# Values of A at the reached half of the far pages' keys only, and those pages' keys read in an order with that half first

## The reference

```
DIL_CFG = ((128, 1), (512, 4), (2048, 16))          # (window, dilation)
for win, dil in DIL_CFG:
    steps = jnp.arange(win // dil + 1) * dil
    kidx = q_idx[:, None] - steps[None, :]          # the keys of this config
    s = einsum(q, k_all[:, kidx]) + bias; s = where(kidx >= 0, s, -inf)
    outs.append(softmax(s) @ v_all[:, kidx])        # then mixed by the denominators
```

## Time and profile before

| | |
|---|---|
| runs | 1401.77, 1408.39, 1410.2 us; median 1408.39 |
| profiled execution | span 1405.5 us, first to last instruction |
| TensorE busy | 1297.9 us, 92% |
| VectorE, ScalarE busy | 550.0 and 257.8 us |
| moved by DMA | 363.80 MB, mean 259 GB/s |

### The profile page before, as it was taken

The page is one execution under the profiler, slowest core; times in us unless marked ns, Lnnn a source line. Parts: engine busy times, 40 slices in busy tenths (PEclk is TensorE's granted clock), DMA queues, the critical chain, the costliest instruction groups (busy, mean ns, idle before and its releaser), DMA issues.

```text
span 1405.5 us, 23104 instructions
## 1 busy us (share of the span) xinstructions
PE 1297.9 (92%) x8038; PEld 816.1 (58%) x8038; DVE 550.0 (39%) x1416; ACT 257.8 (18%) x647; POOL 60.0 (4%) x265
## 2 busy tenths in 40 slices
PE   5989898988899999999999999997879999999998
PEld 2544356645566666666666544665446667767775
DVE  1103787886554101011122088788746511100113
ACT  0111123322213110000004112433211310000001
POOL 1000000000001000000001000000000100000000
PEclk9989999999899999999999999999989999999999
DMA  9988989999843768877863686999993456776663
GB/s 348 239 270 268 284 272 378 322 296 349 283 150 112 274 241 287 316 276 254 333 230 130 202 298 210 332 377 334 348 356 130 142 205 217 242 258 234 210 209 135
DMA packets 189566, 363.80 MB, mean 259 GB/s; under 512 B 22912, under 2 KB 140360, under 8 KB 187786
## 3 DMA queue, kind: packets, MB, share of 16 engines
q1 hardware_dynamic: 155040, 345.62, 71.4%
q10 hardware_dynamic: 34410, 16.70, 4.9%
HBM read 354.17 MB, written 58.40 MB: 294 GB/s over the span
## 4 chain that ended last, share of the span: by engine, by line
PE 67%; DVE 8%; SPq 8%; DMA 7%; DVEq 4%; issue 3%; ACT 2%; ACTq 0%
PE psf L1055 21%; PE psf L1489 19%; SPq L519 7%; DMA ring<-in_tiles 5%; PE psf L1355 4%; PE psf L1401 3%; DVEq L1675 3%; PE psf L1472 3%; DVE m L1672 3%; PE psf L1072 3%; PE psf L1362 2%; PE psf L1102 1%; PE psf L1290 1%; DMA big<-in_pool_cv 1%; PE psf L1134 1%
## 5 line engine op out<-in xcount | busy, mean ns | idle before, releaser
L1055 PE MATMUL psf<-hT,ring 128*128 128x320 f32 x1184 | 329.3, 437 | 2.9 <-DMA ring<-in_tiles 2.7
L1055 PEld LDWEIGHTS psf<-hT,ring 128*128 128x128 f32 x1184 | 224.0, 191 | 111.9 <-issue 15.1
L1489 PE MATMUL psf<-big,ring 128*128 128x320 f32 x1024 | 278.8, 433 | 2.6 <-DVE big L1908 2.1
L1489 PEld LDWEIGHTS psf<-big,ring 128*128 128x128 f32 x1024 | 193.5, 190 | 88.8 <-issue 4.6
L1908 DVE TENSOR_TENSOR big<-sq 128x320 f32<-128x320 f32 x64 | 31.5, 492 | 248.5 <-ACT sq L1024 248.3
L1587 DVE TENSOR_SCALAR rstd<-psf,adaT 128x256 f32<-128x256 f32 x32 | 15.4, 482 | 248.5 <-PE psf L1489 233.3
L1247 PE MATMUL psf<-big,qs 128*32 128x512 f32 x512 | 73.7, 664 | 10.8 <-DVE sel L1877 7.1
L1362 PE MATMUL psf<-hT,ring 128*128 128x320 f32 x224 | 70.3, 459 | 12.2 <-DVE nmxi L1792 12.2
L1672 DVE MAX8 m<-workbuf 64x8 f32<-64x1032 f32 x64 | 78.5, 1227 | 3.5
L1674 DVE MATCH_REPLACE8 workbuf<-m,workbuf 64x1032 f32<-64x1032 f32 x64 | 77.4, 1209 | 0.0
L1355 PE MATMUL psf<-oT,ring 128*128 128x320 f32 x256 | 71.6, 435 | 2.5 <-DMA ring<-in_tiles 1.1
(11 more groups left out here) (192 smaller groups left out, 1255.6 us busy)
## 6 DMA issues: line engine op xcount, KB each, us to landing
ring<-in_tiles SPq DMA_DIRECT2D x272, 512.0 KB, 4.7
big<-in_cache_a SPq DMA_DIRECT2D x64, 768.0 KB, 7.4
out_cache_a<-in_cache_a SPq DMA_DIRECT2D x64, 768.0 KB, 5.8
big<-in_pool_bk SPq DMA_DIRECT2D x128, 192.0 KB, 4.9
big<-in_pool_bv SPq DMA_DIRECT2D x128, 192.0 KB, 6.5
big<-in_pool_cv SPq DMA_DIRECT2D x192, 64.0 KB, 5.9
big<-in_pool_ck SPq DMA_DIRECT2D x128, 64.0 KB, 4.6
big<-in_pool_ck ACTq DMA_DIRECT2D x128, 64.0 KB, 5.3
```

The lines of the kernel that those rows point to most:

```text
L1055: ins = pe.matmul(ps[:, 0:T], ring[:, s, k, :], rhs[:, k, :], start=k == 0, stop=k == KD - 1)
L1489: ins = pe.matmul(bank[6 + m % 2][:, 0:T], ring[:, s, k, :], uT[:, KD * q + k, :], start=q + k == 0, stop=q == 3 and k == KD - 1)
```

## The change

Two things are changed for units of A, in both layers.

First, the values of pages 0 to 3 are loaded in another row order: of each 128 keys first those with a number modulo 16 of 0, then 1, and so on (`reached_first`). For A only the first 64 of these are loaded, on partitions 0 to 63, so this transfer has half the bytes. For C, whose group needs all keys, all 128 rows are loaded in the new order.

Second, everything that meets these values has to be in that order. The logits of pages 0 to 3 are computed with the keys read in it: the moving operand of four matmuls takes a step of 16 elements, in place of adjacent ones. The bias of A, with its mask, is rearranged once, in layer 0, by five copies on VectorE. The outputs of pages 0 to 3 are matmuls over 64 rows for the three groups of A and over 128 for C.

```diff
--- before.py
+++ after.py
@@ -190,6 +190,16 @@
 
     qt, g = n % 2, (6, 0, 1, 2, 7, 3, 4, 5)[n // 2]
     return qt, g, (P if qt == 0 else TP), (2 if g < 6 else 4)
+
+
+
+
+FAR_PAGES = 4
+
+
+def reached_first(ap):
+
+    return ap.rearrange("(a q) w -> q a w", q=16)
 
 
 def repeat(ap, n):
@@ -513,11 +523,11 @@
                                                                  skip_runtime_bounds_check_because=why)
                 return at
 
-            def load_pages(l, at, pool, w0, dst, signal, which=range(NPG)):
+            def load_pages(l, at, pool, w0, dst, signal, which=range(NPG), turned=0):
 
                 for j in which:
-                    sp.dma_start(dst[:, j, :], pool[ds(at[j] + l * N_PHYS, 1), :, w0:w0 + dst.shape[2]]
-                                 .rearrange("o p w -> (o p) w")).then_inc(signal, 16)
+                    src = pool[ds(at[j] + l * N_PHYS, 1), :, w0:w0 + dst.shape[2]].rearrange("o p w -> (o p) w")
+                    sp.dma_start(dst[:, j, :], reached_first(src) if j < turned else src).then_inc(signal, 16)
 
             def load_ik(l, b):
                 load_pages(l, pages(b, CHECKED if l else None), a["pool_ik"], 0, ik[b], ld_ik[b])
@@ -526,16 +536,18 @@
 
                 for e in fours:
                     n, at = A_W // 2, (K_AT, V_AT_)[half]
-                    sp.dma_start(kv[:, u.s, at + n * e:at + n * e + n],
-                                 a["cache_a"][l * NB + u.b, :, half * A_W + n * e:half * A_W + n * e + n]
-                                 ).then_inc((ld_k, ld_v)[half][u.s], 16)
+                    src = a["cache_a"][l * NB + u.b, :, half * A_W + n * e:half * A_W + n * e + n]
+                    dst = kv[:, u.s, at + n * e:at + n * e + n]
+                    if half == 1 and e == 0:
+                        src, dst = reached_first(src)[0:8], dst[0:64]
+                    sp.dma_start(dst, src).then_inc((ld_k, ld_v)[half][u.s], 16)
 
             def load_b(l, u, at, half):
                 load_pages(l, at, a["pool_bv" if half else "pool_bk"], 0, (k_in, v_in)[half][u.s], (ld_k, ld_v)[half][u.s])
 
             def load_c(l, u, at, half, which=range(NPG)):
                 load_pages(l, at, a["pool_cv" if half else "pool_ck"], P * u.second, (ck_in, cv_in)[half][u.s],
-                           (ld_ck, ld_cv)[half][u.s], which)
+                           (ld_ck, ld_cv)[half][u.s], which, FAR_PAGES if half and not u.second else 0)
 
             row = REP * NDIST
 
@@ -1241,6 +1253,8 @@
                             if q < 2:
                                 rhs = (k_in[u.s][:, 4 * q:4 * q + 4, P * c:P * c + P] if c < 3
                                        else ck_in[u.s][:, 4 * q:4 * q + 4, :])
+                                if q == 0 and not u.second:
+                                    rhs = rhs.rearrange("p j (a q) -> p j q a", q=16)
                             else:
                                 rhs = zT[:, u.k + c if c < 3 else u.kc, t0:t0 + NT]
                             masked = u.second and c < 3
@@ -1282,8 +1296,9 @@
                     for j in range(NPG + 1):
                         for c in range(4):
                             if j < NPG:
-                                lhs = PT[:, j, G * c:G * c + G]
-                                rhs = v_in[u.s][:, j, P * c:P * c + P] if c < 3 else cv_in[u.s][:, j, :]
+                                rows = slice(0, 64 if j < FAR_PAGES and c < 3 and not u.second else P)
+                                lhs = PT[rows, j, G * c:G * c + G]
+                                rhs = v_in[u.s][rows, j, P * c:P * c + P] if c < 3 else cv_in[u.s][:, j, :]
                             else:
                                 v0 = u.v + P * c if c < 3 else u.vc
                                 lhs, rhs = PT[0:TS, j, G * c:G * c + G], vs[0:TS, v0:v0 + P]
@@ -1748,6 +1763,14 @@
                         if l == 0:
 
                             dve.wait_ge(ld_dist, N_DIST)
+                            far = slice(0, P * FAR_PAGES)
+                            dve.tensor_copy(S[:, 0, far], sbias[0][:, far])
+                            dve.drain()
+                            for j in range(FAR_PAGES):
+                                page = slice(P * j, P * j + P)
+                                dve.tensor_copy(sbias[0][:, page].rearrange("p (q a) -> p a q", q=16),
+                                                S[:, 0, page].rearrange("p (a q) -> p a q", q=16))
+                            dve.drain()
                         read_logits(UNIT[0])
                     while taken < (made - START[l] - PAIRS) * 2:
                         take8()
```

## The result

| | before | after |
|---|---|---|
| median of the runs timed together | 1407.22 us | 1437.48 us |
| lowest to highest | 1401.77 to 1410.2 | 1433.32 to 1439.48 |
| ratio, with 95% interval | | 1.0228 [1.0199, 1.0257] |
| span of the profiled execution | 1405.5 us | 1431.5 us |

The account below looks back on a forecast made before the run. TensorE, with almost no slack in A units, was taken as the bound, not the loads. Row changes after slack +12.3, bias +0.4 and clock -2.9 us sum to +9.8 on 1408.4, so 1418 us; range 1402 to 1440.

Parts of the forecast that it names:

- The row changes, +1.75 us a unit: Far-page outputs in A units: alternating 64-row and 128-row matmuls take 3.63 against 1.88 us.
- a drain: Far-page outputs: extra time at a change of row count between matmuls; drains alone, as summed, had a chance of 0.38.
- The slack of 12.2 us: TensorE's waits ahead of the late chunk over 14 A units, 12.2 us, subtracted once from the added TensorE work.
- The step of the keys, taken as 0: Logits of pages 0 to 3: reading keys with a step of 16 costs 0; other ends +0.96 and +2.7 us.
- the first rival: Far-page logits in A units: the key step doubles the set, +0.96 us; +24.6 in all, 1433 us; chance 0.27.
- The loads have no share in the pace: A units: no wait there ends with a load, so V's fewer bytes are worth 0 if loads aren't late.
- The clock's dips go, -2.9: Two slow half chunks in layer 0's A units return to normal as waits fill with work: -2.9 us.
- V's transfers in the projection stage, 0 or up to -4.4: Projection stages: halved V transfers don't bring weight tiles sooner, 0; other end 4 transfers at 1.1 us, -4.4 us.
- Bias copies, +0.4: VectorE, layer 0: five copies of 1.3 to 1.9 us, partly in an idle 1.45 us; +0.4, ends 0 and +2.
- SP's queue, 0: SP's issue of loads: still 8 turned C transfers a unit, so the queue's count is unchanged and costs 0.

Follow-up runs that it names:

- e2: Kernel before with only A's outputs of pages 0 to 3 over 64 rows, C's over 128; keys, bias and loads as before: 1.0063, +9 us.
- e5: Kernel before with only the far pages' keys read with a step of 16 and the bias turned; old loads: 1.0026, +3.7 us.
- e6: Kernel before with key step of 16, turned bias and far-page outputs over 64 rows for A, 128 for C; old loads: 1.0153, +21.5 us.
- e16: Kernel before with key step, turned bias and A's twelve 64-row matmuls placed ahead of the rest; old loads: 1.0103, +14.5 us.
- e9: Kernel before with different key steps or output row counts in single A units, wrong values; read from the timeline: steps of 4 to 32 cost 0.87 to 1.0 us.
- e12: Kernel before with V of A's pages 0 to 3 loaded for half of the columns on all 128 partitions: 1.0002, 0 us.
- e8: Kernel before with exactly the changed kernel's loads (A's V on 64 partitions, C's in the new row order), old computation: 1.0165, +23 us.
- e14: Kernel before with only A's V of pages 0 to 3 loaded as 8 x 8 rows to 64 partitions, in the change's order: 1.0131, +18 us.
- e15: Kernel before with only A's V of pages 0 to 3 loaded to 64 partitions in runs of eight adjacent rows, 8 x 8: 1.0125, +18 us.
- e3: Kernel before with V of A's pages 0 to 3 loaded only for partitions 0 to 63, adjacent rows: 1.0058, +8 us.
- e4: The whole change with the twelve 64-row matmuls of a unit first, against the kernel before: 1.0157, +22 us.

## Why the prediction was wrong, point by point

- **The row changes, +1.75 us a unit: right.** 1.72 measured in every A unit, stretch 3.95 for 4.0 forecast, and in the single edit (e2) 9 us where the sum gives 9.0. What the prediction calls a drain is this cost; what TensorE does at such a change no run shows, only the lengths: 3.67 us alternating, 2.94 sorted, 2.09 with 64 rows in all four groups, 1.95 before.
- **The slack of 12.2 us, absorbed once: right.** e5, e2, e6 and e16 all fall within 2 us of the sum that uses it; their intervals are 3 to 5 us wide to either side.
- **The step of the keys, taken as 0: wrong, and the first step that failed.** It doubles the set, +0.88 us (the first rival had +0.96). On top of the row changes no slack hides it: 14 x 0.88 for the loop and twice 0.88 for unit 0 are 14.1 of the 20 us between +9.8 and +30. I argued from a contiguous set that keeps the pace of one stream that the reads had room to spare. The probe shows why this didn't follow: the penalty is each stream's own, so it doesn't show in how many streams run. The nearest row was no evidence about steps at all.
 The doubling in the first rival was an estimate between the two ends of the term. e9 shows it for steps of 4 to 32 (+0.87 to +1.0 us), but not for a step of 2 (+0.05) nor for the order 0, 64, 1, 65 (+0.22); what sets these prices no run shows.
- **"The loads have no share in the pace": wrong as a statement on the change, right on the kernel before.** e12 confirms that the bytes don't matter. What failed is the next thought, and it is the second step that failed: a transfer with another pattern was costed by its bytes alone, C's turned ones by their count, and both put at 0. Loads that had just enough time came late when the same engines moved fewer bytes (286 GB/s in 207:290 of e8, 349 before, at shares of 1.04 and 1.03), and e8 is 23 us by itself. In the change, where TensorE is slower anyway, the loads add 6.4 us by the traces.
 Two prices were missing in that thought. The pattern: 8 x 8 on 64 partitions costs 18 us (e14, e15), one dimension of 64 costs 8 (e3). The partitions: at the same bytes 64 of them cost 8 us (e3), 128 cost 0 (e12).
- **The clock's dips go, -2.9: right in the A units, wrong in sum.** The granted clock is 1.00 in both stretches of A units after, where layer 0 had two dips to 0.50. Two dips came in the projections instead, within waits for weight tiles, and cost 4.1 us.
- **V's transfers in the projection stage, 0 or up to -4.4: wrong in sign.** The program is 3.3 us late at the end of these projections with the change's loads, and 0.9 early without them (e6). I took it that what stands behind a tile in SP's queue doesn't hold it up; the traces of all runs with changed loads are late there.
- **Bias copies, +0.4: hidden**, 1.6 us in all, within the 1.3 to 1.9 forecast, and 0.36 us of waiting is left behind them. **SP's queue, 0:** the count of its issues didn't change and no run speaks against it.

With the measured sizes the prediction's own sum is 14 x 2.60 - 12.2 + 1.8 - 2.9 = +23.1 for TensorE. The loads add 6.4 us in the traces (26.0 less 19.6) and some 8 to 11 in the runs (e4 less e16, the change less e6, each give or take 6), and that is the whole.

That 1437 lies inside the range is in part luck: the range reached so high for the doubled set, and no term of it held the loads. The first rival's 1433 has the right mechanism for TensorE and leaves the loads out as well.

No version tried beats the kernel before. The best that the saved bytes could have brought is e12's 0, and the narrower matmuls save nothing even where all four groups have 64 rows (2.09 us for 1.95).

Open: why the pattern of 16 times 8 rows costs 27 us (V alone) to 36 us while 32 times 4 and 64 times 2 cost nothing. No run here shows which engine gets which rows; that is where one would look next.

## What to carry to other kernels

Work taken away from a resource that no wait ends with brought nothing here, but the way in which it was taken away was still paid: the access patterns had prices of their own, on TensorE and on the DMA engines. When one engine's slack is what hides an edit, sum all edits on that engine before the slack is subtracted, and only once. A busy share of the DMA engines near 1 says that they are occupied, not how much they move (353 GB/s at 1.03 before, 288 at 1.01 after, in layer 0's A units); read GB/s beside it, and treat the first dimension of a pattern (16 x 8 cost 36 us, 32 x 4 none) and the number of partitions (8 us for 64 in place of 128 at the same bytes) as a part of the edit.

## What the runs showed of the hardware that was not expected

- f32 moving operands: a step of 2 elements is nearly free (+0.05 us on a set of 0.88), with steps of 4 to 32 it costs 0.87 to 1.0 more, about a doubling, and in the order 0, 64, 1, 65 it takes 1.10 us. A step of 16 doubles it with 32 columns of the array and with 128 (4.56 for 2.42 us).
- Outputs in which the row count changes from matmul to matmul take 3.67 us for 1.95, with 64 or 32 beside 128: 1.72 more, where the prediction's sum without overlap had 1.75; the same 64 rows in all four groups take 2.09 us.
- Loads of 128 rows of 6 KB at equal bytes, with C's in the same pattern: no cost seen as 64 x 2 and 32 x 4, 36 us as 16 x 8, 68 as 8 x 16, 172 as 4 x 32.
- With half the bytes a load onto 64 partitions is worse for the kernel than the whole one (+8 us), and the engines move 311 GB/s at a share of 1.04; the same bytes over 128 partitions cost nothing, at 320 GB/s and 0.97.
